# Both down projections of a two-block model as seven block products for each pair of output tiles

## The reference, cut to what matters

```python
# first block
f = (jax.nn.silu(h @ w_gate[l]) * (h @ w_up[l])) @ w_down[l]
x = x + gate_f * rmsnorm(f, g_ffn_post[l])
...
# second block
def swiglu(h, w_gate, w_up, w_down):
    return (jax.nn.silu(h @ w_gate) * (h @ w_up)) @ w_down
```

## Time and profile before

| what | value |
|---|---|
| median of three runs | 1657.15 us (1657.09 to 1659.39) |
| profiled execution, first to last instruction | 1655.0 us |
| TensorE matmuls busy | 98% of the span, 9460 instructions |
| VectorE, ACT, POOL busy | 63%, 46%, 44% |
| mean granted clock of TensorE | 0.996 |
| chain that ended last | 90% of it on TensorE |
| first down projection | 467.56 to 591.40 us |
| second down projection | 1520.94 to 1645.65 us |

### The profile page before, as it was taken

The page is one execution under the profiler, slowest core; times in us unless marked ns, Lnnn a source line. Parts: engine busy times, 40 slices in busy tenths (PEclk is TensorE's granted clock), DMA queues, the critical chain, the costliest instruction groups (busy, mean ns, idle before and its releaser), DMA issues.

```text
span 1655.0 us, 24390 instructions
## 1 busy us (share of the span) xinstructions
PE 1628.8 (98%) x9460; PEld 1399.6 (85%) x9460; DVE 1050.5 (63%) x1396; ACT 766.2 (46%) x1029; POOL 732.0 (44%) x540
## 2 busy tenths in 40 slices
PE   7999999999999999999999999999999999999997
PEld 4787899999988898888888887887888789999887
DVE  6777758999920065578778788775113699996102
ACT  4756455455543355334444546544223445544322
POOL 3342343333376635443543434445444443335663
PEclk9999999999999999999999999999999999999999
DMA  8565223333243333233332323223233323332432
GB/s 290 208 225 179 91 89 115 115 105 115 86 150 105 108 115 121 98 102 102 102 105 87 119 85 115 90 90 97 95 112 119 126 83 117 112 111 82 150 97 68
DMA packets 65127, 193.49 MB, mean 117 GB/s; under 512 B 5984, under 2 KB 8288, under 8 KB 64000
## 3 DMA queue, kind: packets, MB, share of 16 engines
q1 hardware_dynamic: 65024, 192.06, 35.3%
HBM read 183.59 MB, written 8.45 MB: 116 GB/s over the span
## 4 chain that ended last, share of the span: by engine, by line
PE 90%; DVE 7%; ACT 1%; issue 1%; DMA 1%; SPq 0%; DVEq 0%
PE PR L778 18%; PE PR L779 18%; PE PR L784 18%; PE PR L1182 4%; PE PR L1189 4%; PE PR L1184 4%; PE AX L1182 3%; PE AX L1189 3%; PE AX L1184 3%; PE PR L795 1%; PE PR L796 1%; PE PR L794 1%; PE AX L1003 1%; PE AX L1330 1%; PE AX L1334 1%
## 5 line engine op out<-in xcount | busy, mean ns | idle before, releaser
L703 POOL TENSOR_TENSOR wlo<-raw,whi 128x512 fp32r<-128x512 f32 (+1 forms) x456 | 605.8, 1354 | 631.3 <-ACT whi L1461 631.3
L1461 ACT ACTIVATE whi<-raw 128x1024 fp32r<-128x1024 f32 x216 | 225.9, 1052 | 150.0 <-PE PR L784 127.2
L778 PE MATMUL PR<-h3h,whi 128*128 128x512 f32 x608 | 245.5, 404 | 0.0
L779 PE MATMUL PR<-h3l,whi 128*128 128x512 f32 x608 | 240.4, 395 | 0.0
L722 POOL TENSOR_TENSOR wlo<-raw,whi 128x512 fp32r<-128x512 f32 x72 | 119.1, 1675 | 239.8 <-ACT whi L1719 239.8
L784 PE MATMUL PR<-h3h,wlo 128*128 128x512 f32 x608 | 154.2, 395 | 0.0
L1182 PE MATMUL PR<-ch,whi 128*128 128x256 f32 x560 | 136.0, 282 | 2.0 <-DVE gate L2509 1.2
L784 PEld LDWEIGHTS PR<-h3h,wlo 128*128 128x128 f32 x608 | 114.2, 188 | 27.6
L778 PEld LDWEIGHTS PR<-h3h,whi 128*128 128x128 f32 x608 | 114.3, 188 | 26.6 <-issue 1.2
L779 PEld LDWEIGHTS PR<-h3l,whi 128*128 128x128 f32 x608 | 114.4, 188 | 26.4 <-issue 1.0
L1184 PE MATMUL PR<-cl,whi 128*128 128x256 f32 x560 | 135.7, 281 | 0.0
(11 more groups left out here) (480 smaller groups left out, 3619.2 us busy)
## 6 DMA issues: line engine op xcount, KB each, us to landing
raw<-w SPq DMA_DIRECT2D x224, 512.0 KB, 3.4
cond<-wcond SPq DMA_DIRECT2D x48, 512.0 KB, 4.2
raw<-w SPq DMA_DIRECT2D x32, 384.0 KB, 3.2
raw<-w SPq DMA_DIRECT2D x32, 320.0 KB, 2.9
x_keep<-x SPq DMA_DIRECT2D x3, 2048.0 KB, 7.3
x<-x_keep SPq DMA_DIRECT2D x2, 2048.0 KB, 8.4
abc_a<-acum_rows SPq DMA_DIRECT2D x8, 512.0 KB, 3.9
abc_b<-acum_rows SPq DMA_DIRECT2D x8, 512.0 KB, 4.5
```

Of the source, the lines that this page charges most:

```text
L703: ins = pool.tensor_tensor(wlo[:, j, a:a + n], raw[:, j, a:a + n], whi[:, j, a:a + n], ALU.subtract)
L778: pe.matmul(bank, whi[:, j, w], part_of(oh, k0 + k), start=first and i == 0, stop=False)
L779: pe.matmul(bank, whi[:, j, w], part_of(ol, k0 + k), start=False, stop=False)
L1461: act.activation(whi[:, j, :], raw[:, j, :], ACT.Copy).then_inc(hi_ready, 1)
```

## The change

Both down projections are made in the block form of the quads. Two output tiles (m, m + 1) form a group, `DN_GROUPS` = 4. Of the 22 k slices, 16 (k 4 to 19, `PAIRS` = 8 even and 8 odd ones) enter 2 x 2 blocks: output tile by even or odd k for the weights, even or odd k by token half for the hidden values. Seven products (A11, A12, A22, S1 to S4) of 24 matmuls of 256 columns make the four output blocks. The other six slices (`ALONE`) stand in two leftover units, O1 and O2, one for each tile, of 6 slices, 3 parts and 2 halves.

Four of the nine low parts of a group are VectorE's (places 0, 1, 3 and 7 of the order), five POOL's (places 2, 4, 5, 6 and 8). VectorE also makes the four sums of weights and, from PSUM, the output blocks; ACT makes all nine high parts and copies A11 out. The group's results alternate between the PSUM tensors AX and PR.

The token side needs sums of hidden values. A third sum (t3) and its low part are made by POOL quad by quad in the block stage, its high part by ACT. The others (t2, t1, t4 and their parts, of 2048 columns each) are made at the start of the down projection, by VectorE, ACT and, for one (`last_low`), POOL. The last group again ends one token half before the other. The loads take every second run of 128 weights, 512 bytes each. For the first block x is now loaded back to another place near the end; for the second it is loaded right behind the first unit O1. The hardware loops of the down stages are gone, all is written out.

The core of the diff:

```diff
-DOWN_K = [(0, 6), (6, 6), (12, 5), (17, 5)]
+PAIRS = 8
+ALONE = (0, 1, 2, 3, 20, 21)
+DN_A = ("A11", "S3", "A12", "S1", "S2", "S4", "O1", "A22", "O2")
+DN_B = ("A11", "S3", "A12", "S2", "A22", "S1", "S4", "O1", "O2")
+DN_GROUPS = KT // 2
+DN_POOL = (2, 4, 5, 6, 8)
+DN_DVE = (0, 1, 3, 7)
...
@@ SP @@
+                half = w22[m].rearrange("p (k two c) -> p k two c", two=2, c=P)[:, 2:10, int(name[2] == "2"), :]
+                sp.dma_start(raw[:, j, :].rearrange("p (k c) -> p k c", c=P), half).then_inc(raw_in[j], 16)
...
+                    dn_free(f, g, "A21")
+                    load_dn(f, g, "O1")
...
+                    if f == 1 and g == 0:
+                        sp.wait_ge(fl_ready, 2 * FT)
+                        sp.wait_ge(s_kept, 48)
+                        sp.dma_start(x[:, :, :], x_keep[:, :, :]).then_inc(s_restored, 16)
+                    if not last:
+                        dn_free(f, g, "A11")
+                        load_dn(f, g + 1, "A21")
+                        dn_free(f, g, "A12")
+                        load_dn(f, g + 1, "A22")
+                    dn_free(f, g, "A22")
+                    load_dn(f, g, "O2")
...
@@ POOL @@
+            def last_low(f):
+                pool.wait_ge(*th_at(f, "b22"))
+                pool.wait_ge(*tp_at(f, "t2"))
+                pool.tensor_tensor(b2l[:, 1, :, :], b2[:, 1, :, :], b22h[:, :, :], ALU.subtract).then_inc(tl_ready, 1)
...
+                for g in range(DN_GROUPS):
+                    for i in DN_POOL:
+                        dn_low(f, g, i)
+                        if g == 0 and i == 2:
+                            last_low(f)
...
@@ TensorE @@
+                dn_product(f, g, "A11")
+                if g == 0:
+                    pe.wait_ge(*tl_at(f, PAIRS - 1))
+                dn_product(f, g, "S3")
+                pe.wait_ge(*one_at(f, g))
+                dn_product(f, g, "A12")
+                if g == 0:
+                    pe.wait_ge(*tp_at(f, "t1l"))
+                dn_product(f, g, "S1")
+                if g == 0:
+                    pe.wait_ge(*tp_at(f, "t2l"))
+                dn_product(f, g, "S2")
+                if g == 0:
+                    pe.wait_ge(*tl_at(f, PAIRS))
+                pe.wait_ge(*dn_step_at(f, g, "p4"))
+                dn_product(f, g, "S4")
+                if g == 0:
+                    pe.wait_ge(fl_ready, FT * (f + 1))
+                dn_alone(f, g, "O1", (0, 1)).then_inc(unit_used, 1)
+                if g == 0:
+                    pe.wait_ge(*tp_at(f, "t4l"))
+                dn_product(f, g, "A22")
+                pe.wait_ge(*dn_step_at(f, g, "two"))
+                dn_alone(f, g, "O2", (0, 1)).then_inc(unit_used, 1)
...
@@ ACT @@
+                dn_ahead(f, 0, 0)
+                token_high(f, "b22")
+                take_one(f, 0)
+                token_high(f, "t1")
+                token_high(f, "t2")
+                dn_ahead(f, 0, 1)
+                quad_gate(QUADS * f + QUADS - 1, 0)
+                dn_ahead(f, 0, 2)
+                quad_ff_high(QUADS * f + QUADS - 1)
...
+                        dn_ahead(f, g, i)
...
+                        if i == 0 and g >= 1:
+                            dn_square(f, g - 1, "c21")
+                            dn_square(f, g - 1, "c22")
+                        if i == 1:
+                            take_one(f, g)
...
@@ VectorE @@
+                if name == "t2":
+                    dve.wait_ge(unit_used, U_DN[f])
+                    dve.wait_ge(*third_at(f, PAIRS - 1, "t1"))
+                    ins = dve.tensor_tensor(t2[:, :, :], b2[:, 1, :, :], b2[:, 0, :, :], ALU.subtract)
...
+            def dn_first(f):
+                end = QUADS * f + QUADS - 1
+                token_part(f, "t2")
+                dn_ahead(f, 0, 0)
+                token_part(f, "t1l")
+                dn_sum(f, 0, "S4")
+                token_part(f, "t4a")
+                token_part(f, "t2l")
+                dn_ahead(f, 0, 1)
+                dn_ahead(f, 0, 2)
+                join(end, 6)
+                quad_ffs(end)
+                quad_ff_low(end)
+                dve.memset(ssum_d[:, :], 0.0).then_inc(dacc, 1)
+                dn_take(f, 0, "p3")
+                dn_take(f, 0, "p4")
+                token_part(f, "t4b")
+                dn_ahead(f, 0, 3)
+                dn_ahead(f, 0, 4)
+                dn_take(f, 0, "two")
+                dn_take(f, 0, "g")
+                token_part(f, "t4l")
...
-            half_x(2, mix2, gffn)
-            down_piece(8)
-            half_h(2, *h_2)
+            half_x(2, mixd, gffn, late_piece, old=x_old)
+            half_h(2, *h_2, late_sum)
```

More of the change, by code:

```diff
@@ L274, in phase_first_quad @@
+        (b1h, b1l, xo_a, xo_b, hth, b2, b2l, t3, t3l, t3h, alone, t2, t4, t2l, t2h, t4l, t4h, sqx, t1h, b22h,
+         one, two, g22, ssum_d, sq_d, wdtr, fh_end, up_2, turn, wdt2, twice) = region(phase_f)
         def phase_first_quad(a):
@@ new lines, in dn_slot, with dn_loaded, dn_sum_at @@
+        def dn_slot(g, name):
+            return ({"A21": 2, "A22": 3, "A11": 0, "A12": 1, "O1": 2, "O2": 3}[name] + 2 * g) % RING
+        def dn_loaded(f, g, name):
+            upto = sum(DN_LOADS[n] for h in range(g + 1) for n in DN_BLOCKS if dn_slot(h, n) == dn_slot(g, name) and (
+                h < g or DN_BLOCKS.index(n) <= DN_BLOCKS.index(name)))
+            return raw_in[dn_slot(g, name)], 16 * (loads(U_DN[f]) // RING + upto)
+        def dn_sum_at(f, g, name):
+            return sum_ready, SUMS_FF * f + 4 * QUADS + 4 * g + ("S1", "S3", "S2", "S4").index(name) + 1
@@ L530, in load_unit @@
             def load_unit(u, j, src):
-                if not isinstance(u, int) or u >= RING and not any(d <= u < d + RING for d in U_DN):
+                if not isinstance(u, int) or u >= RING:
                     sp.wait_ge(lo_ready, u - (RING - 1))
@@ L734, in _ @@
             units(U_GU1 + 4, U_ST1)
[L735 to L737 removed]
+            blocks(0)
             for u in range(U_SC, U_SC + 4):
@@ L742, in _ @@
             units(U_SC + 4, U_ST2)
[L743 to L747 removed]
+            blocks(1)
         @block.tensor
@@ L1138, in _, with dn_operand @@
                     mm.then_inc(unit_used, 1)
-            def down(n, pairs, first_dn, fh, fl, down_taken):
-                wait = banks([down_taken] * 2, nb=2)
-                with pe.Fori(0, pairs) as i:
-                    for b in range(2):
-                        wait(i, b)
-                        for j, (k0, nk) in enumerate(DOWN_K):
-                            if b == 0:
-                                pe.wait_ge(fl_ready, FT * (n - 1) + k0 + nk + (k0 + nk) % 2)
-                            unit(8 * i + (first_dn + 4 * b + j), j, fh, fl, k0, nk, PR[:, DN_BANK[b], :],
-                                 first=j == 0, last=j == 3)
+            def dn_operand(f, name):
+                return {"A11": (b1h[:, 0, :, :], b1l[:, 0, :, :]), "A12": (b1h[:, 1, :, :], b1l[:, 1, :, :]),
+                        "S3": (t3h[f], t3l[f]), "S1": (t1h, b2l[:, 0, :, :]), "S4": (b22h, b2l[:, 1, :, :]),
+                        "S2": (t2h, t2l), "A22": (t4h, t4l)}[name]
```

818 lines of the change are left out of this document (597 added, 221 removed).

## The result

The changed kernel takes 1681.82 us (median of 4 runs, 1681.27 to 1682.85). The kernel before takes 1657.12 us on the same chip (4 runs). The ratio is 1.0151, 95% interval 1.0137 to 1.0166: **slower by 24.7 us**. The profiled execution spans 1681.1 us, 26.1 more than before.

What follows compares the result with a forecast made beforehand. TensorE, busy 98%, bounds the kernel; its saved work is outweighed by waits at the entries. 1655.0 + 8.6 (first projection) + 6.95 (second) + 1.5 (clock) = 1672, median 1674 us; range 1651 to 1684, with 0.56 on 1665 to 1681.

Steps and rivals of the forecast that it cites:

- the slow loads: Rival: loads take 4.5 us or more, the second projection waits 1.2 us per A12; 1682 us or more, chance 0.10.
- TensorE's work: Both down projections: a pair of tiles takes 28.4 us, four pairs 113.6 instead of 123.4; removes 19.6 us in all.
- The entry: Start of each down projection: VectorE and POOL take turns; TensorE waits 3.7, 6.4, 1.6 and 0.3 us.
- POOL's 2048 to 10.0; t1l to 12.2: Entry order in us: POOL's 2048-wide part ends at 10.0, then VectorE's t1l at 12.2; S1 waits 3.7 us.
- 3.5 to 7 was the sign given: Sign of being right: VectorE's 2048-wide parts take 2.2 us alone and 3.5 to 7 in POOL's company.
- The second pair: Wait for A12: 3.4 us for ACT's squares; in the second projection 4.6 for x and 0.5 later.
- The ends: First tail: first mixer matmul at 16.15 us, 2.3 lost; second: 0.95 more, the way to the end as before.
- The clock: Half clock behind the waits of 3.7 and 6.4 us: 0 to 3 us a projection, 1.5 us taken in all.
- the upper bound of 6 us: Clock loss in both projections together if a longer idle between bursts brings the low level.
- What was priced at nothing: Stretches outside the down projections, block stages included: VectorE and POOL stay ahead there, 0 us.
- Faster: Rival: t1l and t2l go before POOL is ready, waits 3.4 and 3.9 us; 1647.5 us, chance 0.17.
- Shared: Rival: VectorE and POOL share at half speed, not in turns, waits 10.7 and 11.5 us; 1663 us, chance 0.13.

Runs made afterwards that it cites:

- the load run: Changed kernel with the four block loads of each pair reading 4 KB in one piece per row, not eight pieces of 512 bytes: 1679.94 us.
- the run with the sums of squares moved: Changed kernel with the first down projection's last two sums of squares issued on VectorE before half h, not inside it: 1678.43 us.
- the run with token copies and two reorderings: Changed kernel, VectorE's six 2048-column token parts as copies, POOL's as zero fill, sums of squares before half h, x restored behind next A21, A22 loads: 1658.94 us.
- three reorderings: Changed kernel with sums of squares before half h, x restored behind the next pair's A21 and A22 loads, A11 copied before ACT's squares: 1666.65 us.

## Why the prediction was right, and where it missed

The sign was right and the time, 1674 us, was 7.8 us too low. It is inside the range, but 0.8 us above the 1665 to 1681 us that had the 0.56, and next to the 1682 us of the slow loads. The number alone would have spoken for that rival, which the load run refutes; only the traces speak for the forecast's mechanism. By its own steps:

**TensorE's work, right.** A product is 2.84 us and the steady pairs run without a pause. All waits of over 0.2 us in the two projections are in the first two pairs or at the ends, but for one of 0.25 us.

**The entry, right in sum and wrong in its order.** The prediction had 3.7 us before S1, 6.4 before S2, 1.6 before S4 and 0.3 before A22, so A22 12.0 us late. It was 12.7 and 12.4 us late. But S1 hardly waited (0.2 us), and S2 waited 9.0 us and ran at half clock. "POOL's 2048 to 10.0; t1l to 12.2" is the sentence that failed. POOL's two parts of A12's low were put from before the entry to 3.9 us; they could only start at 1.3, when ACT's high part was made, and ended at 6.5, just after t1l had started. The long instruction then held the sum for S4 instead. Which of the two went first hung on 0.34 us; what they need together did not, as the run with the instruction in four shows (A22 at 33.9 us again). That the sum fits so well is in part luck, since the predicted order did not happen, and t4a and t2l took 3.4 us in POOL's company where 3.5 to 7 was the sign given. The kernel without that instruction's inputs shows its turn to be the cause of 4.4 and 4.2 us of A22's delay, and the load run that the loads are not. For the rest of the delay the turns are read from lengthened instructions and not tested: no run took all of them away.

**The second pair, right in the first projection and right by its sum in the second.** 3.4 us were priced before A12 of the first projection for ACT's squares, and 3.10 measured. In the second projection 4.6 us were priced at that place, for x, and 0.5 later. Measured were 3.15 us for x, but before O2 of the first pair, where nothing was priced, and 1.91 before A12, again for the squares. The sums, 5.1 and 5.06 us, agree by luck. The run with ACT's copy moved, 9.3 us less, shows that the waits for this copy were no shadow of the entry.

**The ends, right.** Measured down stretch less products, waits and clock: 140.36 - 113.6 - 15.8 - 1.7 = 9.3 us for the first tail, against 16.15 - (113.6 - 106.5) = 9.05. The second: 146.06 - 113.6 - 17.7 - 4.55 = 10.2 against 0.95 + 9.36 = 10.3. That the mixer's first sum stands inside half h and waits was seen ahead, and moving it gave 3.4 us.

**The clock, mis-sized.** "I take 1.5 in all, near the low end, as work returns within 3 us" is the step that failed. 7.75 us of the half clock lay on the path, 6.2 us more than priced. Two things were wrong in it. It looked only behind S1's and S2's waits, and the 5 us there turned out to be the covered ones. And it put nothing behind its own waits of 3.4 and 4.6 us in the second pairs, nor behind the one at the mixer, while the measured ones of 1.91, 3.10, 3.15 and 3.76 us each cost 1.5 to 2.85 us more. Even the upper bound of 6 us was too low.

The Trainium skill, TensorE: Matmul & The Clock Gate, "HAM oscillation", tells of such falls behind longer idle times. The trace agrees at the 9 us waits; behind the shorter ones the measurement decides, and there the clock fell as well.

**What was priced at nothing.** 0.6 us before the first block stage, 0.5 in it, and 0.6 of the 2.1 us in the mixer and second block stage (1.5 is the clock behind the 3.76 us wait). Their cause stays open; the first of them varies by several us between the profiled executions of the kernels above (286.3 to 292.1 us).

Together: 6.2 (clock) + 1.0 (waits) + 0.1 (ends) + 1.7 (unpriced) = 9.0, the difference of 26.1 and 17.05. Between the medians it is 7.8 us only, as the profiled span is 0.7 us under the median of the runs here, where 2.1 were added.

**The rivals.** "Faster" needed the two entries to wait less than 17 us together; they wait 18 us before S2 alone. Half of its condition came true: t1l did go ahead of POOL's long instruction, but what stood behind it was held. "Shared" needed 10.7 and 11.5 us of waits in all, and both projections have more (15.8 and 17.7). "Loads too slow" fell by the load run: faster loads took 1.9 us off and left S2's waits as they were.

## What to carry to other kernels

When work for VectorE and POOL is added ahead of a point that TensorE waits for, add up both engines' instructions on SBUF as one queue up to the first operand needed; the split and the length of the instructions move the waits about and hardly their sum. Then allow for 1.5 to 3 us of half clock behind every wait of about 2 us or more on TensorE, except where what comes next waits anyway. That is what most such waits cost in these traces; a few cost nothing, so it is a range and no fixed price. Last, look in each engine's queue for small steps (here two squares, a restore, two additions) that stand ahead of something TensorE needs: three reorderings gave 15.2 of the 24.7 us back.

## What was not expected of the hardware

- VectorE's copies with a single SBUF input are held by POOL's operations too: 2.28 to 2.32 us for 2048 columns beside POOL's four weight parts, 1.22 us alone. The Trainium skill, SBUF — State Buffer, "SBUF: two separate sides", counts fast-mode operations of VectorE among those that need the shared port pair; the trace agrees.
- The clock fell behind single waits of 1.91, 2.39 and 3.10 us in work that was otherwise dense. The length of the wait does not settle it: the clock stayed at 1.00 behind 3.19 us in the second projection of the run with the sums of squares moved, and behind 2.39 and 2.03 us in the load run; it fell behind the same 1.46 us wait in the run with token copies and two reorderings, and not in the run with the sums alone. What decides between them, no run here shows. The wait of 3.19 us with the window behind it, then the window behind the 1.46 us wait (at 597.21) that was followed by a fall:

```profile
1586.16 0.39 PE L1378 MATMUL PR<-b1h,whi 128*128 128x256 f32 x1 [3.19 <-ACT one L2099]
...
1588.00:1590.00 2.00, 2.00 (x19) 1.00 0.85 244
```

```profile
600.00:602.00 2.00, 2.00 (x11) 0.50 0.04 8
```

- 2048 columns on POOL took 6.62 us in VectorE's company, where four times its 1.27 us for 512 gives 5.1: it began 0.34 us after t1l, which ran for 2.53.
